# The two token halves of a decoder's expert layer change roles, and expert numbers are looked up on GpSimd

## What is computed

```python
qry = (xt @ w_query).reshape(PEER_BLOCK, PEER_HEADS, 2, PEER_KEY_DIM)
s1 = jnp.einsum('thd,kd->thk', qry[:, :, 0], keys1)      # 8 heads, 128 keys
s2 = jnp.einsum('thd,kd->thk', qry[:, :, 1], keys2)
v1, i1 = lax.top_k(s1, PEER_TOPK)                        # 16 of 128
v2, i2 = lax.top_k(s2, PEER_TOPK)
cand_s = (v1[..., :, None] + v2[..., None, :]).reshape(PEER_BLOCK, PEER_HEADS, PEER_TOPK * PEER_TOPK)
cand_i = (i1[..., :, None] * PEER_KEYS + i2[..., None, :]).reshape(...)
top_s, pos = lax.top_k(cand_s, PEER_TOPK)                # 16 of 256 pairs
idx = jnp.take_along_axis(cand_i, pos, axis=-1)
gate = jax.nn.softmax(top_s, axis=-1)
act = jax.nn.gelu(jnp.einsum('td,thkd->thk', xt, expert_u[idx]))
out = jnp.einsum('thk,thkd->td', gate * act, expert_v[idx])
```

## Time and profile before

| | us |
|---|---|
| median of 3 runs | 4370.32 (4368.96 to 4373.33) |
| the profiled execution's own time | 4365.77 |
| its span, first to last instruction | 4364.0 |
| PE busy in the span | 3831.0 (88%) |
| DVE busy | 2714.0 (62%) |
| POOL busy | 1636.7 (38%) |
| ACT busy | 912.6 (21%) |
| mean granted TensorE clock | 0.936 |

### The profile page before, as it was taken

How to read it: one execution, slowest core, us unless ns; L and a number is a source line. 1 busy time by engine, 2 the same in 40 slices (tenths; PEclk the granted TensorE clock), 3 DMA queues, 4 the chain that set the end, 5 groups by cost and what they waited for, 6 DMA issues and landing times. The chain is left out here.

```text
span 4364.0 us, 43792 instructions
## 1 busy us (share of the span) xinstructions
PE 3831.0 (88%) x15856; PEld 2832.5 (65%) x15856; DVE 2714.0 (62%) x5304; ACT 912.6 (21%) x1953; POOL 1636.7 (38%) x1552
## 2 busy tenths in 40 slices
PE   8789999967999999994797899999679999999937
PEld 7546787856766666652684467888567666666516
DVE  4865216658567666777658651165685676667775
ACT  2243302236200000000122532021461000000001
POOL 6612000023355555566375120000243554555563
PEclk9789999988999999997897899999899999999968
DMA  2001233348899999999620012333579999999996
GB/s 100 29 29 39 74 135 124 121 173 294 323 390 401 403 392 410 375 410 403 250 80 29 30 39 84 135 123 125 193 278 340 391 400 403 394 409 376 410 383 253
DMA packets 300550, 1063.83 MB, mean 244 GB/s; under 512 B 41648, under 2 KB 75056, under 8 KB 274992
## 3 DMA queue, kind: packets, MB, share of 16 engines
q0 software_dynamic: 147456, 536.94, 32.0%
q1 hardware_dynamic: 119312, 488.44, 29.5%
q10 hardware_dynamic: 33568, 35.65, 2.3%
HBM read 1025.27 MB, written 35.65 MB: 243 GB/s over the span
## 5 line engine op out<-in xcount | busy, mean ns | idle before, releaser
L2040 POOL DMA_INDIRECT u_rows<-in_peer_u,idx_all x512 | 663.9, 1297 | 1652.3 <-DVEq L1943 933.2
L1647 PE MATMUL bank<-v_tile,shared 128*128 128x512 f32 x2048 | 906.1, 597 | 14.2 <-DVE shared L1990 13.9
L1963 DVE SCALAR_TENSOR_TENSOR x<-v_rows,act_w,x 128x1024 f32<-128x1024 f32 x512 | 657.6, 1284 | 206.1 <-DMA v_rows<-in_peer_v,idx_all 176.1
L2040 POOL DMA_INDIRECT v_rows<-in_peer_v,idx_all x512 | 587.7, 1148 | 453.9 <-DVE x L1963 337.8
L1647 PEld LDWEIGHTS bank<-v_tile,shared 128*128 128x128 f32 x2048 | 391.8, 192 | 467.2 <-issue 444.6
L1951 DVE CUSTOM_DVE_ANT_0 u_rows<-u_rows,h 128x1024 f32<-128x1024 f32 x512 | 605.8, 1223 | 99.1 <-DMA u_rows<-in_peer_u,idx_all 98.2
L1635 PE MATMUL bank<-hT,bT 128*128 128x256 f32 x2048 | 452.5, 379 | 0.0
L1635 PEld LDWEIGHTS bank<-hT,bT 128*128 128x128 f32 x2048 | 388.4, 190 | 72.0 <-issue 22.0
L1538 PE MATMUL bank<-hT,ring 128*128 128x256 f32 x1536 | 341.0, 383 | 14.4 <-PEq L150 14.4
L1538 PEld LDWEIGHTS bank<-hT,ring 128*128 128x128 f32 x1536 | 293.6, 192 | 56.7 <-issue 16.0
L1817 ACT ACTIVATE shared<-bank 128x512 f32<-128x512 f32 x128 | 76.2, 595 | 1023.4 <-PE bank L1647 948.7
(11 more groups left out here) (362 smaller groups left out, 5311.2 us busy)
## 6 DMA issues: line engine op xcount, KB each, us to landing
v_tile<-in_peer_v SPq DMA_DIRECT2D x256, 512.0 KB, 7.2
ring<-in_w_in_panels SPq DMA_DIRECT2D x76, 1024.0 KB, 4.8
bT<-in_peer_ut SPq DMA_DIRECT2D x128, 512.0 KB, 7.3
ring<-in_peer_w_query SPq DMA_DIRECT2D x32, 1024.0 KB, 4.8
aT<-in_peer_ut SPq DMA_DIRECT2D x64, 512.0 KB, 6.7
sT<-in_peer_ut SPq DMA_DIRECT2D x64, 512.0 KB, 7.2
gates<-dense_gates SPq DMA_DIRECT2D x32, 1024.0 KB, 10.7
ring<-in_ple_w_gate SPq DMA_DIRECT2D x24, 1024.0 KB, 7.6
```

The lines of the kernel that those rows point to most:

```text
L1647: ins = mm(acc[t][part][:, :], act_pair[p % AHEAD][:, at:at + P], v_tile[:, e % DENSE, part * 512:part * 512 + 512], start=(e == 0), stop= ...
L1963: stt(out=m.x[:, 2 + t, :], in0=vr[:, n % RINGS, :], scalar=act_w[:, p % 4, i:i + 1], in1=m.x[:, 2 + t, :], op0=ALU.mult, op1=ALU.add).the ...
L2040: nc.gpsimd.indirect_dma_start(out=rows[:, n % RINGS, :], out_offset=None, in_=table, in_offset=bass.IndirectOffsetOnAxis(ap=idx_all[:, t, ...
```

## The change

The halves swap roles. The first half now gathers, the second goes densely.

- In the list, each of the first half's choices from head 1 on is followed by a chunk (7 chunks), beside the second half's `gate`, `mix` and now also `out` steps. Then all eight choices of the second half follow one another, each with a chunk and a `pre` behind it, then `slots`, the 64 `hot` steps with 8 chunks and four `pre` steps, and the 64 pairs with the rest. `DENSE_END` is 59.
- Only 54 of the 256 candidate pairs are formed, in five groups by rank (`RANKS`): rank a of the first list with rank b of the second for which (a+1)(b+1) is at most 16, and a few more. The selection runs over 54.
- VectorE only compares the 32 positions with a ramp of 54 (1728 elements, into `gates`). GpSimd forms the 54 expert numbers, multiplies them with the comparison, and adds the 54 up in halving steps (`choose` on GpSimd). It does this ahead of the chunk's gathers, in list order. VectorE waits in choice k until choice k-2 is decoded.
- `slots` waits until all 16 choices are decoded, and splits the numbers on VectorE with five instructions.
- `score` waits on the chosen count alone; `hot` takes its operands' places from `gain_ffn`, `scores` and `query`, so that all twelve pair buffers are free for early `pre` steps.

```diff
-DENSE_END = 58
+RANKS = (0, 1, 16), (1, 2, 8), (2, 4, 5), (4, 8, 3), (8, 16, 1)
+CANDS = sum((hi - lo) * n for lo, hi, n in RANKS)
+DENSE_END = 59
@@ tail_order
         order += [("choose", head, part) for part in (2, 3)]
-        if head >= 2:
+        order.append(next(second))
+        if head:
+            order.append(("chunk", next(chunks)))
+        if head % 2 == 0:
             order.append(next(second))
     order += list(second)
-    order += [("norm", 1), ("query", 1, 0), ("query", 1, 1), ("score", 1, 0)]
-    order += [("choose", PEER_HEADS, part) for part in range(4)]
-    order += [("score", 1, 1), ("slots",)]
...
+    order += [("norm", 1), ("query", 1, 0)]
+    pairs = iter(range(AHEAD))
+    for head in range(PEER_HEADS):
+        if head + 1 < PEER_HEADS:
+            order.append(("query", 1, head + 1))
+        order.append(("score", 1, head))
+        order += [("choose", PEER_HEADS + head, part) for part in (0, 1)]
+        order.append(("pre", next(pairs)))
+        order += [("choose", PEER_HEADS + head, part) for part in (2, 3)]
+        order.append(("chunk", next(chunks)))
+    order.append(("slots",))
     for q in range(QUADS):
         order.append(("hot", q))
         if q % (QUADS // HOT_CHUNKS) == QUADS // HOT_CHUNKS - 1:
-            order += chunk(q // (QUADS // HOT_CHUNKS))
-        if q % 10 == 9 and pairs < EARLY:
+            order.append(("chunk", next(chunks)))
+        if q % 16 == 12:
+            order.append(("pre", next(pairs)))
@@ vector, choose part 3
+                    step.step(nc.vector.tensor_copy(posf[:, :, :], pos[:, :, :]))
+                    tt(hit[:, k % 2], over(posf[:, :, :]..., (P, 2 * TOPK, CANDS)),
+                       over(m.c("iota")[:, 0:CANDS].unsqueeze(1), (P, 2 * TOPK, CANDS)), ALU.is_equal).then_inc(s.ranked, 1)
@@ gpsimd
+            def choose(k, part):
...
+                pool.wait_ge(s.ranked, k + 1)
+                for lo, hi, n in RANKS:
+                    step.mark(tt(cand_id[...], over(vif[:, k % 2, :, 0, lo:hi]...), over(vif[:, k % 2, :, 1, 0:n]...), ALU.add))
+                for t in range(2):
+                    step.mark(tt(mine[:, t], mine[:, t], over(cand_id[:, t].unsqueeze(1), (P, TOPK, CANDS)), ALU.mult))
+                width = CANDS
+                while width > 2:
+                    low = width // 2
+                    step.step(tt(hit[:, k % 2, :, 0:low], hit[:, k % 2, :, 0:low], hit[:, k % 2, :, width - low:width], ALU.add))
+                    width -= low
+                step.step(tt(dsel[:, 1, :, some] if half else ids[:, :, :], mine[:, :, :, 0], mine[:, :, :, 1], ALU.add))
+                pool.sem_inc(s.decoded, 1)
```

More of the change, by code:

```diff
@@ L1353, in tail_order @@
     second = iter(steps[1])
+    chunks = iter(range(CHUNKS + 2))
     for head in range(PEER_HEADS):
@@ L1385, in tail_order @@
         if q % (QUADS // HOT_CHUNKS) == QUADS // HOT_CHUNKS - 1:
-            order += chunk(q // (QUADS // HOT_CHUNKS))
-        if q % 10 == 9 and pairs < EARLY:
-            order.append(("pre", pairs))
-            pairs += 1
+            order.append(("chunk", next(chunks)))
+        if q % 16 == 12:
+            order.append(("pre", next(pairs)))
     order.append(("hot", QUADS))
-    for p in range(pairs, AHEAD):
-        order.append(("pre", p))
-    done = 0
-    for c in range(HOT_CHUNKS, CHUNKS + 2):
-        goal = min(PAIRS_ALL, -(-(c - HOT_CHUNKS + 1) * PAIRS_ALL // (DENSE_END - HOT_CHUNKS)))
+    order += [("pre", p) for p in pairs]
+    done, first = 0, next(chunks)
+    for c in range(first, CHUNKS + 2):
+        goal = min(PAIRS_ALL, -(-(c - first + 1) * PAIRS_ALL // (DENSE_END - first)))
         for p in range(done, goal):
@@ L1400, in tail_order @@
         done = goal
-        order += chunk(c)
+        order.append(("chunk", c))
         if c == DENSE_END:
@@ L1765, in score @@
             def score(half, head):
-                if half and head >= 4:
-                    act.wait_ge(s.selected, head - 3)
-                elif half or head >= 4:
-                    act.wait_ge(s.dsel_ready, head + 5 if half else head - 3)
+                if half or head >= 4:
+                    act.wait_ge(s.picked, PEER_HEADS * half + head - 3)
                 bank = banks.take()
@@ L1882, in choose @@
                 lists = [(t, a) for t in range(2) for a in range(2)]
-                cf = [cand[:, t].rearrange("p a b -> p (a b)") for t in range(2)]
+                cf = [cand[:, t] for t in range(2)]
                 if part == 0:
@@ L1930, in choose @@
-                    h5 = hit[:, :, :].rearrange("p (a t k) n -> p a t k n", a=2, t=2)
-                    for a in range(2):
-                        step.mark(tt(h5[:, a], h5[:, a], over(vif[:, :, a, :].unsqueeze(2), (P, 2, TOPK, TOPK)), ALU.mult))
-                    step.settle()
                     some = slice(head * TOPK, (head + 1) * TOPK)
-                    for a in range(2):
-                        step.mark(nc.vector.tensor_reduce(chosen[:, a] if half else dsel[:, a, :, some], h5[:, a], AX_X, ALU.add))
+                    step.step(nc.vector.tensor_copy(posf[:, :, :], pos[:, :, :]))
@@ L1937, in choose @@
+                    tt(hit[:, k % 2], over(posf[:, :, :].rearrange("p t k -> p (t k)").unsqueeze(2), (P, 2 * TOPK, CANDS)),
+                       over(m.c("iota")[:, 0:CANDS].unsqueeze(1), (P, 2 * TOPK, CANDS)), ALU.is_equal).then_inc(s.ranked, 1)
                     v.wait_ge(s.exp_done, 2 * k + 2)
                     step.step(nc.vector.reciprocal(rden, den))
-                    if half:
-                        step.step(stt(out=chosen[:, 0], in0=chosen[:, 0], scalar=float(KEYS), in1=chosen[:, 1], op0=ALU.mult, op1=ALU.add))
-                        step.mark(ts(idx_all[:, :, some], chosen[:, 0], float(layer * EXPERTS), None, ALU.add))
@@ L2021, in embedded @@
                 tt(xs, xs, ple_sig[:, n, at].rearrange("p (t c) -> p t c", t=len(UNITS[unit])), ALU.add).then_inc(s.ple_added, 1)
-            parts = {"mix": mix, "out": out, "norm": norm, "choose": choose, "chunk": chunk, "hot": hot, "values": values, "add": add,
+            parts = {"mix": mix, "out": out, "norm": norm, "choose": choose, "slots": slots, "chunk": chunk, "hot": hot, "values": values, "add": add,
                      "embed": embed, "turn": turn, "embedded": embedded}
@@ L2053, in _ @@
                     fetch(n, s.v_free, vr, tables[1], m.v_landed)
+            parts = {"choose": choose, "chunk": chunk}
+            for what, *n in order:
+                if what in parts:
+                    parts[what](*n)
     clear(nc, s)
```

120 lines of the change are left out of this document (66 added, 54 removed).

## The result

The changed kernel takes **4592.0 us** (median of 4 runs, 4589.8 to 4593.9), the kernel before 4370.4 us: a ratio of 1.0506, 95% interval 1.0488 to 1.0524. It is slower by 222 us. The forecast was 4525 us, range 4440 to 4640.

A forecast was written before the change was run, and what follows sets the result against it. TensorE was taken to set the pairs, transfers close behind. Stage terms summed to +77.3 us a layer, +155 for two; on 4365.8 that is 4520, plus 4.5 for the runs' median gives 4525 us, range 4440 to 4640.

The forecast's parts named there:

- likeliest case: Main forecast: second-half choice cycles of 24 to 28 us, giving 4480 to 4590 us; chance 50%.
- The second half's choices: Norm to first `hot`: seven more cycles of 25.5 us, set by GpSimd, make the stage +192.5 us a layer.
- lower bound: One GpSimd look-up, estimated from elementwise rows: 10.0 us.
- case without contention: Rival, 18%: look-up takes its 10.0 us, cycle 22.2, +42.2 us per layer, 4454 us.
- full alternation: Rival, 22%: GpSimd and VectorE alternate, look-up 19 us, cycle 31, +131.8 us per layer, 4634 us.
- upper bound: One GpSimd look-up if every instruction waits for one of VectorE's: 19 us.
- The choices beside the mixing: First half's choices stage: GpSimd's cycle and lock waits 14 us, chunk 6 before the norm 10.2; +24 us a layer.
- `hot`: The `hot` stage: one choice, a query, a score and two blocking `pre` steps go; 173 us, −22.3 a layer.
- pairs: The 64 pairs: five queries and scores and end waits go; TensorE sets 794 us, −48.4 a layer.
- Store to first `values`: Last gates store to first `values`: loads follow the store's landing, 17.3 + 10 = 27.3 us, −20.3 a layer.
- Last `values` to `add`: Wait behind the pairs: gathers no longer late, 1 us left of 46.2, −45.2 a layer.
- Behind `add`: After `add`: same order with one chunk fewer at the very end, −3 us a layer.

The follow-up runs named there:

- `a_cut`: Changed kernel with GpSimd's look-up cut short: two multiplications and six halvings left out, as many rows gathered; 4446.6 us.
- `a_no2`: Changed kernel with no chunk among the second half's eight choices, those eight chunks moved into the pairs; 4464.3 us.
- `a_no1`: Changed kernel with no chunk beside the first half's choices, those seven chunks moved to the pairs; 4528.8 us.
- `a_dve`: Changed kernel with the look-up of the numbers on VectorE in place of GpSimd; 4591.6 us.
- `b_half`: Kernel before with every gathered row cut to 512 of its 1024 columns, in the transfer and VectorE's two operations; 4334.0 us.
- `a_time`: Changed kernel with the pairs' chunks laid out by TensorE's time, half as many for the last 12 pairs; 4598.0 us.
- `b_time`: Kernel before with its 50 chunks of the pairs laid out by TensorE's time, no other change; 4331.5 us.
- `b_gap_time`: Kernel before with three chunks moved to the six products before the first `values`, and the pairs' chunks laid out by TensorE's time; 4309.1 us.
- `b_gap`: Kernel before with three chunks of the pairs moved to the six first-stage products between last `hot` quad and first `values`; 4378.3 us.
- `a_no2_time`: Changed kernel without chunks in the second half's choices, and with the pairs' chunks laid out by TensorE's time; 4371.5 us.

## Why the prediction was right, and where its sum was off

The direction, the place and the mechanism were right; the sum was 67 us short for two layers (222 measured, 155 forecast; 37.7 by the table for layer 0). 4592.0 us lies in the range and 2 us above the band given for the likeliest case, 4480 to 4590. The errors of the two mis-sized stages that came out shorter than forecast, 3.5 and 5.8 us, hid a part of the others.

- **The second half's choices** (+192.5 forecast, +203.1 measured). A cycle of 25.5 us was forecast, with look-ups of 12 to 15; the profile has 26.4 and 13.5. GpSimd sets it; without most of the look-up it is VectorE's 21.5 (21.4 forecast). `a_cut` (−44 us) and `a_no2` (−90 us) show both parts. The lower bound of 10.0 us for a look-up was right (10.1 with no chunk beside it, in `a_no1`). The case without contention falls with the v additions, 1841 against 1284 ns, and with the look-up's 13.5 us; full alternation falls with the same 13.5, which are not 19. That upper bound doesn't come out of its rows: the nine long instructions of a chunk and a comparison are 12 us by them, so 22 and not 19. The rule of the Trainium skill, "SBUF — State Buffer", section "SBUF: two separate sides", that one of the two engines keeps the shared ports for an instruction's whole length, agrees with the stretched v additions, 1841 against 1284 ns. How often the two meet set the size here.
- **The choices beside the mixing** (+24, +32.8). The step was right in kind: 14 us were put down to GpSimd's cycle and VectorE's waits for the lock. `a_cut` and `a_no1` each take the growth away. What they take away is VectorE's time, set down as 171 us and measured as 197.4: `a_dve`, in which GpSimd forms no numbers and VectorE is as busy with its own look-up, has the same long stage. So the length does not need the lock. What the two kernels have in common is a VectorE that is busy for as long; in the changed kernel it is the stretching that fills it. Its u products took 1729 ns there, and chunk 6 ahead of the norm took 16.6 us, where 10.2 had been set down.
- **`hot`** (−22.3, −25.8) and **pairs** (−48.4, −48.1): right. `b_half` shows that TensorE, not the gathers, sets the pairs.
- **Store to first `values`** (−20.3, −26.1): mis-sized. The gates' loads were issued 12.7 us behind the store, not 17.3, so 21.5 us in place of 27.3.
- **Last `values` to `add`** (−45.2, −21.6): the term that was mis-sized most, 23.6 of the 37.7 us a layer. The prediction compared bytes and time over the whole pairs, 287 MB and 794 us, and concluded that the gathers are no longer late. But the last 12 pairs take only 77 us of TensorE's time and got 36/64 × 12 = 6.75 chunks and their own weights, 42 MB (410 GB/s × 102 us). `a_time` shows it, with 0.6 us left.
- **Behind `add`** (−3, +0.7): nothing came.

## What to carry to other kernels

Before work is moved out of a stage, ask which engine covers it there: of seven choices, six stood beside TensorE's pairs, where it waited for only 6.4 us in all; in front of everything each of the seven cost 16 us without a chunk and 29 us with one ((145.1 − 32.4) / 7 and (235.4 − 32.4) / 7). A stage average of bytes against time hides its end: where the bounding engine's work for each step changes, lay the transfers out by that engine's time, and not by steps. For two lines of the order it gave 0.8% (`b_time`), 1.6% (`b_gap_time` against `b_gap`) and 2.1% (`a_no2_time` against `a_no2`); in `a_time` it took the wait away as well, but two other stages grew by as much. Moving elementwise work from VectorE to GpSimd paid nothing here, where both engines read SBUF at the same time; no run shows what it does where they don't.
